# Zero products taken out of two attentions of a three-block network on one core

## The chip, the core and the metric

The kernel runs on one NeuronCore of one Trainium2 chip. Five engines matter: TensorE (PE) multiplies, VectorE (DVE) and ScalarE (ACT) work element by element, GpSimd (POOL) does a few additions and fills, and SyncE (SP) issues the loads. The metric is the device time of one execution in microseconds; the lower the better. The time of the kernel before is 1631.91 us, the median of three runs.

## What is computed

A sequence of 256 positions and 1024 channels passes a first block of two layers (an even mixer of convolutions, an odd mixer of a linear recurrence and a dilated attention, each followed by a gated feed-forward) and a second block of two layers (feed-forward, a mixer of pooling and a latent attention, feed-forward). All numbers are 32 bits wide. Cut to what the change touches:

```python
def dilated_attention(q, k, v, q_norm_g, k_norm_g):      # once, in the odd layer
    for g, (window, dilation) in enumerate(((128, 1), (512, 4), (2048, 16))):
        o, lse = dilated_group_attention(qn[:, :, g], kn[:, :, g], vr[:, :, g], window, dilation)
    ...
    out = jnp.einsum("gbsh,gbshd->bshd", softmax(lses), outs)

def mla_attention(...):                                   # twice, in each layer of the second block
    s = (einsum('bhqd,bhkd->bhqk', qn_b, kn) + einsum('bhqd,bkd->bhqk', qr_b, k_rope)) * SOFTMAX_SCALE
    s = jnp.where(qpos[:, None] >= kpos[None, :], s, -jnp.inf)
    p = jax.nn.softmax(s, axis=-1)
    return jnp.einsum('bhqk,bhkd->bhqd', p, vv)
```

## The kernel before

Activations stay in the core's memory; 343 MB of weights stream past them. Every unit of weights (mostly 128 x 2048 numbers) is loaded into `raw`, copied by ACT to a rounded high part `wh` and subtracted by DVE to a low part `wl`, and PE multiplies with both. Each engine has its own program, written out by hand; semaphores order them, and within an engine the work runs in the order in which it is written. Nothing is scheduled by a planner.

The dilated attention runs in three rounds: round 0 is the first 128 positions with four heads, rounds 1 and 2 are the second 128 positions with two heads each. Per round the stations are:

- `scores(r)` on PE, line 824: 6 products of 128 x 256 or 12 of 128 x 128;
- on DVE the mask (line 1705), the row maximum (line 1712) and its negative (line 1713);
- on ACT the exponentials (line 1191); on DVE the reciprocal (line 1723) and the scaling (line 1726), which give the probabilities;
- `turn(r)` on PE, line 835: 12 transposes; on ACT the copy of what they give (line 1201);
- `values(r)` on PE, line 846: 12 products of probabilities and values; on ACT the copy of the result (line 1348).

PE's program runs them as scores 0, half a unit of the output projection (line 738), scores 1, turn 0, scores 2, values 0, turn 1, values 1, turn 2, values 2, then the rest of the output projection (lines 738 and 646). DVE works through mask 1, probabilities 1, the low part of one weight unit (line 1490), mask 2, probabilities 2.

The latent attention has two rounds with the same stations (its mask is line 1708, its last copy line 1442). There half units of the output projection stand between the stations: scores 1, turn 0, half a unit, values 0, half a unit, turn 1, values 1, half a unit and the rest.

The function `spin(n, bk)` (line 671) multiplies a 128 x 128 tile of zeros `ZB` (16-bit numbers) with itself four times side by side, n times over, into a bank of the accumulator memory that is written afresh afterwards. Nothing reads what it writes. It is called in two places at the beginning (8 and 14 products), ahead of values 0, 1 and 2 of the dilated attention (3, 4 and 4 products) and ahead of values 1 of each latent attention (3 products), 39 in all. The spin calls in the attentions stand in front of the wait of `values` for ACT's copy (`_turned`).

Of the kernel before, what the change touches and what calls it, by code (L numbers as in the profile page):

```python
# [261 lines left out]
def build(nc, A, const, out):  # L262

    ctx = ExitStack()
    with ctx:
# [43 lines left out]
        def bank(i, a=0, n=512, rows=slice(0, P)):  # L309
            return PS[rows, i, a:a + n]  # L310
# [15 lines left out]
        def pairs(ap, w=S):  # L326
            return ap.rearrange("p (t s) -> p t s", s=w)

        def over(ap, n):

            return ap.unsqueeze(1).to_broadcast([ap.shape[0], n, ap.shape[1]])
# [38 lines left out]
        def ev(name):  # L370

            if name not in events:
                events[name] = sem("ev_" + name)
            return events[name]
# [229 lines left out]
        def _(pe):  # L604
# [66 lines left out]
            def spin(n, bk=5):  # L671

                for _ in range(n):
                    mm(pairs(bank(bk), P), lhsT=ZB[:], rhs=over(ZB[:], 4), start=True, stop=True)
# [279 lines left out]
            scores(1)  # L954
            turn(0)
            scores(2)
            spin(3, 7)
            values(0)
            turn(1)
            pe.wait_ge(ev("dil_taken"), 1)  # L960
            spin(4, 7)
            values(1)
            turn(2)
            pe.wait_ge(ev("dil_taken"), 2)
            spin(4, 7)
            values(2)
            half_unit(od, 6, "y_od", True, 6)
            for u in range(1, 4):
# [4 lines left out]
            for l in range(2):  # L973
# [65 lines left out]
                half_unit(n0 + 1, 5, fill, False)  # L1039
                turn(1)  # L1040
                pe.wait_ge(ev("y_pool"), 4 * l + 4)
                spin(3, 7)
                values(1)
                half_unit(n0 + 2, 6, fill, False)
                for u in range(3):
# [1117 lines left out]
```

## Time and profile before

| | |
|---|---|
| median of the runs | 1631.91 us (1629.73, 1631.91, 1632.4) |
| the profiled execution | 1632.11 us, of which its span is 1630.3 us |
| PE busy | 1595.9 us, 98% of the span |
| DVE busy | 1262.8 us, 77% |
| ACT busy | 854.8 us, 52% |
| mean granted clock of PE | 0.997 |
| zero products in the trace | 39, of them 22 at the beginning, 11 in the dilated attention (from 444.9 us), 3 in each latent attention |

The span is the time from the first to the last instruction; 1.81 us of the profiled execution lie around it. The granted clock is 1.00 at 2.4 GHz and 0.50 at 1.2 GHz. A busy PE in the profile has its matmuls overlapping: one of 12 that follow each other is shown with its whole latency, so the pace is read from where the next group starts. In the trace a product of two 32-bit tiles has two records, hence x24 for 12 products, while transposes have one each.

### The profile page before, as it was taken

To read this page: it belongs to the slowest core of one execution; us is meant where nothing else is said; L and a number is where in the kernel's file an instruction comes from. 1 tells how busy PE (TensorE), PEld (TensorE's weight loads), DVE (VectorE), ACT (ScalarE), POOL (GpSimd) and SP (SyncE) were. 2 spreads that over 40 slices of the span, in tenths; PEclk is the share of its full clock that TensorE was granted. 3 is DMA by queue.
4 is the path that set the end of the run, shared out by engine and by line. 5 is a ranking of instruction groups with operands and counts; after the bars stand their busy time and mean duration, and the time that the engine had idled before them with its cause. 6 is when DMAs were issued, how large, how long until landed. Compare 5 with 4: busy or idle time off the path is not lost.

```text
span 1630.3 us, 26968 instructions
## 1 busy us (share of the span) xinstructions
PE 1595.9 (98%) x11041; PEld 1453.5 (89%) x11041; DVE 1262.8 (77%) x1449; ACT 854.8 (52%) x1025; POOL 56.7 (3%) x76
## 2 busy tenths in 40 slices
PE   8999999999989999999999999999999999999998
PEld 7989999888789999899999799999899998899997
DVE  6977889886768898778888777885878888685555
ACT  5556645555356554654446565444644455564443
POOL 3001000000010000000000010000000000010000
PEclk9999999999999999999999999999999999999999
DMA  7514888744236886488974348876498854266562
GB/s 246 181 52 155 298 316 292 254 152 136 65 128 235 324 290 197 140 291 309 306 249 141 128 140 305 305 259 193 140 320 316 309 182 159 80 192 194 180 189 82
DMA packets 231438, 343.65 MB, mean 211 GB/s; under 512 B 7066, under 2 KB 194048, under 8 KB 231360
## 3 DMA queue, kind: packets, MB, share of 16 engines
q1 hardware_dynamic: 230304, 341.11, 62.0%
q0 software_dynamic: 752, 1.18, 0.2%
q8 instruction: 55, 0.90, 0.2%
q10 hardware_dynamic: 304, 0.27, 0.1%
q14 instruction: 23, 0.19, 0.0%
HBM read 341.48 MB, written 1.05 MB: 210 GB/s over the span
## 4 chain that ended last, share of the span: by engine, by line
PE 76%; DVE 11%; issue 5%; ACT 5%; SPq 1%; DMA 0%; DVEq 0%; ACTq 0%
PE PS L666 21%; PE PS L768 20%; PE PS L667 11%; PE PS L646 9%; PE PS L624 4%; DVE wl L1490 4%; PE PS L738 2%; ACT wh L1069 2%; PE PS L633 2%; PE PS L694 2%; PE PS L895 2%; DVE Z L1589 1%; DVE XL L1506 1%; PE PS L824 1%; SPq L521 1%
## 5 line engine op out<-in xcount | busy, mean ns | idle before, releaser
L1490 DVE TENSOR_TENSOR wl<-raw,wh 128x2048 fp32r<-128x2048 f32 (+2 forms) x256 | 570.4, 2231 | 153.5 <-ACT wh L1069 151.5
L666 PE MATMUL PS<-HP,wh 128*128 128x512 f32 x1728 | 607.8, 395 | 0.0
L1069 ACT ACTIVATE wh<-raw 128x2048 fp32r<-128x2048 f32 (+2 forms) x256 | 475.6, 1859 | 139.9 <-PE PS L768 117.0
L667 PE MATMUL PS<-HP,wl 128*128 128x256 f32 x1728 | 484.2, 280 | 0.0
L666 PEld LDWEIGHTS PS<-HP,wh 128*128 128x128 f32 x1728 | 324.1, 188 | 74.7 <-DVE wl L1490 0.3
L768 PE MATMUL PS<-FX,wh 128*128 128x256 f32 x1920 | 345.1, 281 | 1.8 <-DVE FX L1655 1.8
L667 PEld LDWEIGHTS PS<-HP,wl 128*128 128x128 f32 x1728 | 326.4, 189 | 0.0
L768 PEld LDWEIGHTS PS<-FX,wh 128*128 128x128 f32 x1920 | 294.7, 188 | 4.4 <-DVE wl L1490 2.0
L768 PE MATMUL PS<-FX,wl 128*128 128x256 f32 x960 | 269.9, 281 | 0.0
L768 PEld LDWEIGHTS PS<-FX,wl 128*128 128x128 f32 x960 | 180.7, 188 | 0.0
L1589 DVE SCALAR_TENSOR_TENSOR Z<-ada,CA,Z 128x1024 f32 x126 | 161.3, 1280 | 1.3
L646 PE MATMUL PS<-HP,wh 128*128 128x256 f32 x848 | 156.9, 287 | 3.0 <-issue 1.9
L624 PE MATMUL PS<-FX,wh 128*128 128x258 f32 (+2 forms) x576 | 142.2, 286 | 5.5 <-ACT FX L1081 3.6
L646 PEld LDWEIGHTS PS<-HP,wh 128*128 128x128 f32 x848 | 133.6, 194 | 9.4 <-issue 4.7
L624 PE MATMUL PS<-FX,wl 128*128 128x258 f32 (+2 forms) x576 | 140.0, 282 | 0.0
L1135 ACT ACTIVATE WK<-PS 128x512 f32<-128x512 f32 x54 | 32.3, 598 | 197.0 <-PE PS L667 197.0
L646 PE MATMUL PS<-HP,wl 128*128 128x256 f32 x424 | 119.3, 284 | 0.0
L624 PEld LDWEIGHTS PS<-FX,wh 128*128 128x128 f32 (+1 forms) x576 | 108.1, 188 | 10.5 <-ACT FX L1081 5.3
L624 PEld LDWEIGHTS PS<-FX,wl 128*128 128x128 f32 (+1 forms) x576 | 108.2, 188 | 0.0
L1160 ACT ACTIVATE WK<-PS 128x512 f32<-128x512 f32 x54 | 32.0, 593 | 97.0 <-PE PS L667 96.9
L646 PEld LDWEIGHTS PS<-HP,wl 128*128 128x128 f32 x424 | 81.7, 193 | 0.0
L633 PE MATMUL PS<-XL,wh 128*128 128x256 f32 (+1 forms) x576 | 75.5, 283 | 0.0
(281 smaller groups left out, 1724.5 us busy)
## 6 DMA issues: line engine op xcount, KB each, us to landing
ada<-ada_w SPq DMA_DIRECT2D x144, 512.0 KB, 6.2
raw<-ffn_w_gate SPq DMA_DIRECT2D x66, 1024.0 KB, 5.4
raw<-ffn_w_up SPq DMA_DIRECT2D x66, 1024.0 KB, 5.5
raw<-ffn_w_down SPq DMA_DIRECT2D x66, 1024.0 KB, 5.0
raw<-od_w_in SPq DMA_DIRECT2D x13, 1024.0 KB, 5.3
raw<-ev_w_in SPq DMA_DIRECT2D x10, 1024.0 KB, 7.2
raw<-w_in SPq DMA_DIRECT2D x8, 1024.0 KB, 5.4
raw<-w_out SPq DMA_DIRECT2D x8, 1024.0 KB, 6.1
```

Source lines behind the costliest of these rows:

```text
L624: mm(bank(dst + m, 0, width, slice(0, rows[m])), lhsT=w(a, k, m * P, rows[m]), rhs=XH[:, k, 0:width], start=k == 0 and a == 0, stop=False, ...
L633: last = mm(bank(dst + m, 0, S, slice(0, rows[m])), lhsT=w(0, k, m * P, rows[m]), rhs=XL[:, k, :], start=False, stop=k == KD - 1, skip_gro ...
L646: last = mm(dst, lhsT=lhs(a, k), rhs=rhs(b, k), start=first and i == 0, stop=first and i == len(order) - 1, skip_group_check=not first)
L666: mm(pairs(bank(bk)), lhsT=lhs(0, k), rhs=HP[:, k], start=k == 0, stop=False, skip_group_check=True)
L667: last = mm(bank(bk, 0, S), lhsT=lhs(1, k), rhs=HH[:, k, :], start=False, stop=k == k_tiles - 1, skip_group_check=True)
L694: last = mm(bank(bk + h, 0, 512, slice(0, 4)), lhsT=cn("pick")[:, 3 - v:7 - v], rhs=Z[:, at + v * D + 512 * h:at + v * D + 512 * h + 512], ...
L738: last = mm(bank(bk, m * S, S), lhsT=w(a, k, m * P, P), rhs=H[b][:, k, :], start=m == 0 and k == 0 and i == 0, stop=False, skip_group_chec ...
L768: last = mm(bank(m // 2, (m % 2) * S, S), lhsT=w(a, k, m * P, P), rhs=rhs(b, k), start=begins and i == 0 and m % 2 == 0, stop=False, skip_ ...
L895: mm(bank(4 + t // 2, (t % 2) * S, S), lhsT=DG[:, i % DIAGS, :], rhs=cols(Z, EV["U"], 4, 30 + S)[:, t, k:k + S], start=k == DVE_TAPS, stop ...
L1069: last = A_(dst(wh), src, ACT.Copy)
L1490: last = tt(dst(wl), src, dst(wh).bitcast(F32), ALU.subtract)
L1589: ins = stt(total, w, CA[:, k:k + 1], total, ALU.mult, ALU.add)
```

## The change

Five calls of `spin` go: those before values 0, 1 and 2 of the dilated attention and the one in the loop over the two latent attentions. The 22 zero products at the beginning stay. Waits, orders and all other instructions stay as they are.

```diff
@@ dilated attention, PE
             scores(1)
             turn(0)
             scores(2)
-            spin(3, 7)
             values(0)
             turn(1)
             pe.wait_ge(ev("dil_taken"), 1)
-            spin(4, 7)
             values(1)
             turn(2)
             pe.wait_ge(ev("dil_taken"), 2)
-            spin(4, 7)
             values(2)
             half_unit(od, 6, "y_od", True, 6)
@@ latent attention, PE, in the loop over two layers
                 half_unit(n0 + 1, 5, fill, False)
                 turn(1)
                 pe.wait_ge(ev("y_pool"), 4 * l + 4)
-                spin(3, 7)
                 values(1)
                 half_unit(n0 + 2, 6, fill, False)
```

On PE in the dilated attention the row of instructions changes as follows (`PS` is the accumulator memory, `CN` holds the identity for transposes, `WK` the probabilities, `Z` queries, keys and values, `ZB` the zeros):

```order
 L835 MATMUL PS<-CN,WK 128x128 x12
 L824 MATMUL PS<-Z 128x256 x6
-L674 MATMUL PS<-ZB 128x512 x3
 L846 MATMUL PS<-WK,Z 64x128 x12
 L835 MATMUL PS<-CN,WK 128x128 x12
-L674 MATMUL PS<-ZB 128x512 x4
 L846 MATMUL PS<-WK,Z 64x128 x12
 L835 MATMUL PS<-CN,WK 128x128 x12
-L674 MATMUL PS<-ZB 128x512 x4
 L846 MATMUL PS<-WK,Z 64x128 x12
```

Three groups of zero products are gone, one in front of each `values`; nothing else has moved. On PE in each latent attention one group is gone between turn 1 and values 1 (`HP` holds the activations of the output projection):

```order
 L738 MATMUL PS<-HP,wl 128x256
 L835 MATMUL PS<-CN,WK 128x128 x8
-L674 MATMUL PS<-ZB 128x512 x3
 L846 MATMUL PS<-WK,Z 128x128 x8
 L738 MATMUL PS<-HP,wh 128x256 x2
```

The transposes are now followed directly by the products of the values, which wait for ACT's copy of the transposes.

## Rows read from the trace of the kernel before

**Rows 1.** The page: the span, and the shares of the chain that ended last.
```profile
span 1630.3 us, 26968 instructions
...
PE 76%; DVE 11%; issue 5%; ACT 5%; SPq 1%; DMA 0%; DVEq 0%; ACTq 0%
```

**Rows 2.** Zero products after 100 us: ns min/median/max, first and last start.
```profile
L674 PE MATMUL PS<-ZB x17: 379/379/379, 445.1 to 1412.0; 128*128 128x512 bf16 x17
```

**Rows 3.** Timeline, PE, dilated attention: start us, length us, what, [idle before <- releaser].
```profile
434.01 2.75 PE L824 MATMUL PS<-Z 128*128 128x256 f32 x12
439.41 1.97 PE L835 MATMUL PS<-CN,WK 128*128 128x128 f32 x12 [2.65 <-DVE WK L1726]
441.18 4.06 PE L824 MATMUL PS<-Z 128*128 128x256 f32 x12
445.08 0.81 PE L674 MATMUL PS<-ZB 128*128 128x512 bf16 x3
445.82 1.80 PE L846 MATMUL PS<-WK,Z 128*64 128x128 f32 x24
447.55 1.53 PE L835 MATMUL PS<-CN,WK 128*128 128x128 f32 x12
448.92 1.03 PE L674 MATMUL PS<-ZB 128*128 128x512 bf16 x4
450.62 2.46 PE L846 MATMUL PS<-WK,Z 128*64 128x128 f32 x24 [0.68 <-ACT WK L1201]
455.12 1.53 PE L835 MATMUL PS<-CN,WK 128*128 128x128 f32 x12 [2.04 <-DVE WK L1726]
456.49 1.03 PE L674 MATMUL PS<-ZB 128*128 128x512 bf16 x4
458.19 2.46 PE L846 MATMUL PS<-WK,Z 128*64 128x128 f32 x24 [0.68 <-ACT WK L1201]
462.56 0.47 PE L738 MATMUL PS<-HP,wh 128*128 128x256 f32 x2 [1.92 <-DVE HP L1556]
```

**Rows 4.** Timeline, ACT, dilated attention: the three copies of the transposes.
```profile
441.42 1.45 ACT L1201 ACTIVATE WK<-PS 128x1536 f32<-128x1536 f32 x1 [3.72 <-PE PS L835]
...
449.12 1.45 ACT L1201 ACTIVATE WK<-PS 128x1536 f32<-128x1536 f32 x1 [1.08 <-PE PS L835]
...
456.69 1.45 ACT L1201 ACTIVATE WK<-PS 128x1536 f32<-128x1536 f32 x1 [2.85 <-PE PS L835]
```

**Rows 5.** Timeline, DVE, dilated attention: between probabilities 1 and probabilities 2.
```profile
446.29 1.75 DVE L1490 TENSOR_TENSOR wl<-raw,wh 128x1536 fp32r<-128x1536 f32 x1
447.96 1.75 DVE L1705 TENSOR_TENSOR WK<-PS,CN 128x1536 f32<-128x1536 f32 x1
...
453.91 1.15 DVE L1726 TENSOR_SCALAR WK<-WK,SM 128x768 f32<-128x768 f32 x2
```

**Rows 6.** Windows of PE: stretch, length, busy (instructions), granted clock, DMA share, GB/s.
```profile
440.00:444.00 4.00, 4.00 (x16) 0.57 0.00 0
...
452.00:456.00 4.00, 1.96 (x20) 1.00 0.17 56
456.00:460.00 4.00, 3.32 (x30) 1.00 0.00 0
```

**Rows 7.** Timeline, latent attentions: round 1 of the first, then of the second.
```profile
933.85 0.81 PE L674 MATMUL PS<-ZB 128*128 128x512 bf16 x3
...
935.13 2.05 PE L846 MATMUL PS<-WK,Z 128*128 128x128 f32 x16 [0.47 <-ACT WK L1201]
...
1411.52 0.81 PE L674 MATMUL PS<-ZB 128*128 128x512 bf16 x3
1411.72 1.02 ACT L1201 ACTIVATE WK<-PS 128x1024 f32<-128x1024 f32 x1 [2.67 <-PE PS L835]
...
1412.80 2.05 PE L846 MATMUL PS<-WK,Z 128*128 128x128 f32 x16 [0.47 <-ACT WK L1201]
```

**Rows 8.** Windows behind the dilated attention: busy of PE, PEld, DVE, ACT, POOL; granted clock.
```profile
463.00:473.00 10.00, 10.00 (x86) 10.00 (x85) 6.31 (x7) 6.07 (x9) 2.02 (x2) 1.00 0.34 107
```

## The prediction

> **What bounds the kernel now.** I read the page first: the span is 1630.3 us, and the chain that ended last lies on PE for 76% of it [rows 1]. So PE's work counts where PE waits for nobody, and the question for each of the 17 zero products taken out [rows 2] is whether the engine had something else to do at that moment. The timeline of PE through the dilated attention tells that [rows 3]: behind the second and third group of zero products PE still sits idle for 0.68 us until ACT has copied the transposes, and in the latent attentions it sits idle for 0.47 us behind its group [rows 7]. Then I read the timelines of ACT and DVE beside it [rows 4, 5], which say what ends each wait, and last the granted clock in the windows [rows 6], since PE's clock is what such products can influence without anybody reading them. Behind the attention PE runs without a gap (10.00 of 10.00 us busy [rows 8]), so whatever delays the start of the output projection at 462.56 us is passed on whole.
>
> **The price of one zero product.** Three in a row take 0.81 us and each has 0.379 us of latency [rows 2, 3], so the pace is (0.81 - 0.379) / 2 = 0.216 us. Four in a row give (1.03 - 0.379) / 3 = 0.217 us. Seventeen are 17 x 0.216 = 3.7 us of PE; that they were all on the path would be the most the removal could give.
>
> **Group 1, ahead of values 0 (3 products).** ACT's copy for values 0 ended at 441.42 + 1.45 = 442.87 us [rows 4], long before values 0 started at 445.82 us. So this group really holds PE up: without it values 0 starts where the zeros started, at 445.08 us, 0.74 us earlier, and turn 1 at 446.81 instead of 447.55 us. Its probabilities are ready for that, because DVE goes on to its next work at 446.29 us, at the end of them [rows 5]. ACT's copy, which started at 449.12 us, then starts about 1.6 us (449.12 - 447.55) behind turn 1, at 448.38, and ends at 449.83 us; values 1 can start at 449.88 instead of 450.62 us. What is late next? Turn 2 waits for probabilities 2, and these come from a chain on DVE and ACT that starts with the mask at 447.96 us, directly behind the low part of a weight unit that starts at 446.29 us [rows 5]. The mask needs scores 2, which ended before 445.3 us (441.18 + 4.06) [rows 3], and nothing in it waits for values 0, turn 1 or values 1. So turn 2 stays at 455.12 us, and the 0.74 us end as idle time of PE. The term is 0.
>
> **Groups 2 and 3, ahead of values 1 and 2 (4 products each).** Values 2 starts at 458.19 us, directly behind ACT's copy (456.69 + 1.45 = 458.14 us [rows 3, 4]). The zeros ended at 457.52 us, beside that copy. Removing them changes nothing on the path: turn 2 (455.12), copy (456.69), values 2 (458.19), the last copies, projection (462.56) keep their times. The same for group 2, with 450.57 us as the end of the copy. The term is 0 for both; the cover is ACT's copy of 1.45 us against 0.87 us of zeros.
>
> **Latent attentions (3 products each).** The copy ends at 1411.72 + 1.02 = 1412.74 us and values 1 starts at 1412.80 us, while the zeros were over at 1412.33 us [rows 7]. The first layer has the same rows around 934 us, with the same 0.47 us of idle time. The term is 0 for both, and PE is idle there from the start of the copy to values 1 instead, 1412.80 - 1411.72 = 1.1 us, between projections on either side.
>
> **The clock.** Taken so far the sum is 0, and what remains is what the zeros do to the clock. In this trace it fell to 0.57 in the window 440 to 444 us, that is to the 1.2 GHz level for most of it [rows 6], right behind an idle time of 2.65 us in front of turn 0 [rows 3]. It did not fall in the windows of 452 to 460 us [rows 6], where the idle times are 0.68, 2.04, 0.68 and 1.92 us [rows 3]. The change opens just these: values 1 moves forward by 0.74 us while turn 2 stays, so the idle time before turn 2 becomes 2.04 + 0.74 = 2.78 us, longer than the 2.65 us that stood before the fall; the waits for ACT's copy become 458.19 - (455.12 + 1.53) = 1.54 us instead of 0.68. From the end of turn 1 to the projection PE then works for 2.46 + 1.53 + 2.46 = 6.45 us of about 14.2. One more fall here is therefore possible in many executions, and this trace can't say in which.
>
> Its price: at half the clock scores 2 took 4.06 us where the same products at 434.01 us took 2.75, so 1.31 us; turn 0 took 1.97 us where turn 1 and turn 2 took 1.53, so 0.44 us; together 1.75 us [rows 3]. There it cost nothing, since DVE's mask came at 447.96 us only, 2.7 us behind scores 2. In round 2 the work between waits is on the path. The ends are 0 (no further fall, or one that falls into idle time) and 1.75 us for each one, at most two of them between 452 and 470 us, 3.5 us. I take 0.44 us, the excess of turn 0, because the work that stands right behind the lengthened idle time is a turn of the same form, and because a good part of a slow stretch lies in waits. Below nothing there is no clock term: the one fall of before is off the path.
>
> The Trainium skill speaks against the change (TensorE: Matmul & The Clock Gate, section "HAM oscillation — how this bites in real kernels"): bursts of matmuls with waits between them lose the full clock again and again, and the extra time is the throttled time multiplied by (1 - 1.2/2.4). The rows agree on the size: 4.06 + 1.97 us of slowed work cost 1.75 us, of which not all ran slow. By that rule every thinned attention would pay; this is the second rival below.
>
> **The sum.** 1632.11 us of the profiled execution, plus 0 for the five groups, plus 0.44 us for the clock, is 1632.5 us. The profiled execution stands 0.2 us above the median of 1631.91 us, so no correction is worth making.
>
> **Rivals.** (1) The zeros were holding nothing, and the clock falls no more often than before. For it: the clock stayed at 1.00 over 2.04 and 1.92 us of idle time; against it: 2.78 us is beyond the 2.65 us behind which it fell in this attention. The time is 1632.1 us. (2) Slower: the clock falls twice or more on the path. The place is round 2 of the dilated attention and the start of the projection, with idle times of 2.78, 1.54 and 1.92 us close to each other, and perhaps the latent attentions too. Two falls give 1632.1 + 3.5 = 1635.6 us, three 1637.4 us. It decides from the second full fall on. Against it: in the latent attentions only 1.1 us of idle time opens between dense work, and any slow stretch after 462.56 us is met by the dense work of the projection, and dense work is what lifted the clock again here after the fall at 440 us: it was at 1.00 by 452 us [rows 6]. (3) Faster: the zeros did stand in the way, because the next real product isn't free to start while they drain, or because executions differ in when ACT's copy ends. All 17 on the path give 0.74 + 2 x 0.87 + 2 x 0.65 = 3.8 us and 1628.3 us. Against it speak four idle times behind the zeros, 0.68 and 0.47 us, in front of the very products that would be freed [rows 3, 7].
>
> **How the numbers follow.** The forecast, hidden zeros and at most one fall on the path, has 0.66, rival 1 has 0.18, rival 2 has 0.11, rival 3 has 0.05. A measurement of this kernel can tell about 0.2% from no change, that is 3.3 us; forecast and rival 1 lie within it. Of rival 2 I count 0.10 as slower by more than that, of rival 3 0.04 as faster, and 0.86 remain. The range goes down to the lowest run of before, 1629.7 us, since nothing but rival 3 is below it, and up to two falls, 1635.6 us.
>
> **What the profile after would show.** Values 0 follows scores 2 directly. The idle time before turn 2 longer, near 2.8 us, and turn 2 still released by DVE line 1726. Values 2 and both late `values` of the latent attentions released by ACT line 1201, with idle times near 1.5 and 1.1 us. The stretch from probabilities 1 to the start of the output projection (446.3 to 462.56 us, 16.3 us) unchanged where the clock stays at 1.00, longer by up to 1.75 us where it shows 0.50. The forecast is wrong if the projection starts earlier relative to probabilities 1, or if the clock is low in two or more places where it was full before.

## The result

The changed kernel takes 1635.86 us, the median of 12 executions (1632.15 to 1639.27), beside 1632.34 us for the kernel before in the same series (12 executions, 1629.73 to 1636.66). The ratio is 1.0019 with a 95% interval of 1.0010 to 1.0028: slower by about 0.2%. Two more series of the same kernel gave 1.0001 (0.9991 to 1.0011) and 1.0000 (0.9987 to 1.0012). Taken together the mean of 35 executions of the changed kernel is 1634.7 us and that of 98 of the kernel before is 1633.6 us, so the removal costs 1.1 us, with a 95% interval of 0.2 to 2.0 us. This leans on the first series: one by one the means differ by 3.5, 0.4 and 0.3 us, and the last two alone don't tell the removal from nothing. In the first series the kernel before also had only one of 12 executions above 1634.5 us, against 33 of 86 in the others. Four executions of over 1700 us (one of the changed kernel, three of the kernel before) are left out of all means here.

The profiled execution of the changed kernel took 1633.50 us, with this span on the page, to be held against [rows 1]:

```profile
span 1631.7 us, 26936 instructions
```

The timeline of PE through the dilated attention (start us, length us, what, [idle before <- releaser]) answers to [rows 3]. The line numbers of ACT and DVE are lower by four than before, as the calls are gone.

```profile
433.55 2.75 PE L824 MATMUL PS<-Z 128*128 128x256 f32 x12
438.96 2.47 PE L835 MATMUL PS<-CN,WK 128*128 128x128 f32 x12 [2.66 <-DVE WK L1722]
441.22 3.54 PE L824 MATMUL PS<-Z 128*128 128x256 f32 x12
444.69 1.80 PE L846 MATMUL PS<-WK,Z 128*64 128x128 f32 x24
446.42 1.53 PE L835 MATMUL PS<-CN,WK 128*128 128x128 f32 x12
449.54 2.43 PE L846 MATMUL PS<-WK,Z 128*64 128x128 f32 x24 [1.58 <-issue]
454.88 1.53 PE L835 MATMUL PS<-CN,WK 128*128 128x128 f32 x12 [2.91 <-DVE WK L1722]
457.99 2.43 PE L846 MATMUL PS<-WK,Z 128*64 128x128 f32 x24 [1.59 <-issue]
462.33 0.48 PE L738 MATMUL PS<-HP,wh 128*128 128x256 f32 x2 [1.92 <-DVE HP L1552]
```

Values 0 follows scores 2 directly, the three zero groups have become idle time, and turn 2 still waits for DVE. The idle times of 1.58 and 1.59 us are put down to `issue` and not to ACT, but ACT's copy ends right before each: the last one starts at 456.44 us and takes 1.45, which is 457.89 us, 0.10 us before values 2. From scores 1 to the output projection it is 462.33 - 433.55 = 28.78 us, where it was 462.56 - 434.01 = 28.55 us before [rows 3]. Up to there the removal of 11 products has changed 0.23 us, and to the worse. The stretch that the prediction named, from the end of probabilities 1 to the projection, starts with this line of DVE:

```profile
446.05 1.75 DVE L1486 TENSOR_TENSOR wl<-raw,wh 128x1536 fp32r<-128x1536 f32 x1
```

It is 462.33 - 446.05 = 16.28 us, before it was 462.56 - 446.29 = 16.27 us [rows 3, 5]: unchanged. What follows is new. The windows of PE (stretch, length, busy and records, granted clock, DMA share, GB/s) right behind the start of the projection, which [rows 8] shows at 1.00 throughout:

```profile
462.00:464.00 2.00, 1.67 (x11) 0.82 0.03 8
464.00:466.00 2.00, 2.00 (x12) 0.50 0.00 0
466.00:468.00 2.00, 2.00 (x16) 0.83 0.00 0
468.00:470.00 2.00, 2.00 (x19) 1.00 0.33 68
```

PE starts 12 matmuls in 2 us at the lower clock against 19 at the full one. What that costs is seen at the first product behind the output projection, before and then after:

```profile
477.03 0.28 PE L624 MATMUL PS<-FX,wh 128*128 128x256 f32 x1
```
```profile
478.30 0.28 PE L624 MATMUL PS<-FX,wh 128*128 128x256 f32 x1
```

From the start of the projection it took 477.03 - 462.56 = 14.47 us, now it takes 478.30 - 462.33 = 15.97 us: the fall of the clock cost 1.50 us. The values 1 of the latent attentions come here:

```profile
936.50 2.02 PE L846 MATMUL PS<-WK,Z 128*128 128x128 f32 x16 [1.21 <-ACT WK L1197]
...
1414.19 2.02 PE L846 MATMUL PS<-WK,Z 128*128 128x128 f32 x16 [1.21 <-ACT WK L1197]
```

Against [rows 7] they are late by 936.50 - 935.13 = 1.37 and 1414.19 - 1412.80 = 1.39 us. Between the two nothing more was lost. Of the 1.37 us, 1.27 were there at 478.30 us already, and the other 0.1 us is new in the latent attention: values 1 starts 0.15 us behind the end of ACT's copy, where it was 0.06 us. The spans differ by 1.4 us. In this pair of executions the changed kernel reached scores 1 0.46 us earlier, lost 0.23 us in the attention, 1.50 us to the fall in the projection, and 0.1 us in the latent attention.

### The profile page after: what moved, and what is told of

Its sections match the earlier page's. It is cut to its first block, busy times and chain, and to the rows that moved or that the text cites. A ratio compares the mean times of both kernels' runs of the same rounds, so it can differ in the third digit from the quotient of the medians.

```text
span 1631.7 us, 26936 instructions
## 1 busy us (share of the span) xinstructions
PE 1592.5 (98%) x11024; PEld 1453.7 (89%) x11024; DVE 1263.1 (77%) x1449; ACT 854.7 (52%) x1025; POOL 56.6 (3%) x76
## 3 DMA queue, kind: packets, MB, share of 16 engines
HBM read 341.48 MB, written 1.05 MB: 210 GB/s over the span
## 4 chain that ended last, share of the span: by engine, by line
PE 76%; DVE 11%; issue 5%; ACT 5%; SPq 1%; DMA 0%; DVEq 0%; ACTq 0%
PE PS L666 21%; PE PS L768 20%; PE PS L667 11%; PE PS L646 9%; PE PS L624 4%; DVE wl L1486 4%; PE PS L738 2%; ACT wh L1065 2%; PE PS L633 2%; PE PS L694 2%; PE PS L895 2%; DVE Z L1585 1%; DVE XL L1502 1%; SPq L521 1%; PE PS L824 1%
```

## The experiments

Theory: the removed products were hidden behind waits and cost nothing, and what they did was to keep PE's clock full; without them it falls more often at places of the path. Rivals: the latent attentions pay as well; the difference has nothing to do with the clock; the zeros hold nothing. Besides the medians, each execution's mean clock is used.

**One part alone.** The label dil_only leaves the 11 products of the dilated attention out:

```diff
-            spin(3, 7)
             values(0)
...
-            spin(4, 7)
             values(1)
...
-            spin(4, 7)
             values(2)
```

> Only the 11 zero products of the dilated attention are taken out, the 6 of the latent attentions stay. Theory (clock falls in the dilated attention and at the start of its output projection): the whole slowing of the change is here, 2.5 to 4 us above the kernel before, and the runs have a lower mean clock, 0.991 to 0.996. Rival (the latent attentions pay too): 1 to 2 us, about half. Rival (something else than the clock, such as the placement of the code): a difference of time without one of the clock.

Measured: 1633.86 us, ratio 1.0002 (0.9992 to 1.0013), mean 1634.3 against 1633.6 us. The size was missed. The clock went from 0.991 to 0.997, but its mean, 0.9946 against 0.9954, is hardly lower; one of 12 executions (1639.39 us, 0.991) has a lower clock and a longer time than any of the kernel before. The label lat_only leaves out the other 6:

```diff
                 pe.wait_ge(ev("y_pool"), 4 * l + 4)
-                spin(3, 7)
                 values(1)
```

> Only the 6 zero products of the latent attentions are taken out, the 11 of the dilated attention stay. Theory: no difference from the kernel before, within 1 us, since only 1.1 us of idle time opens there between dense stretches. Rival (the latent attentions pay too): 1 to 2 us slower, with falls of the clock near 935 or 1413 us in some executions.

Measured: 1633.04 us, ratio 0.9994 (0.9985 to 1.0004). The means differ by 0.1 us with an uncertainty of 1.1 us, no execution stands out, and in the profile the clock is 1.00 around both latent attentions. So they pay nothing that can be measured here.

**The changed kernel again.**

> The changed kernel once more, for a second profile and for each run's mean clock beside its time. Theory: 2.5 to 4 us above the kernel before, and run by run the time rises by about 1.6 us for each 0.001 that the mean clock is lower (0.001 of 1632 us), since every slowed product is on the path. Rival (the extra time has nothing to do with the clock): no such relation.

Measured: 1633.24 us, ratio 1.0001; the size was missed again. The relation held in kind: over the 12 executions the time rises by 1.05 us for each 0.001 of mean clock, in the first series by 1.26 us, and by 1.26 and 1.20 us over 35 and 31 executions of the kernel before. The executions of the changed kernel of 1638.67 us and above all have a clock of 0.991. The code is the same in each of these, so its placement doesn't make their difference.

> The changed kernel a third time, for a tighter comparison. So far its medians stood 3.5 and 0.05 us above the kernel before in two series. Theory (the removal costs nothing where the clock is full, and lets it fall once more on the path in a part of the executions): a mean 0.5 to 2 us above the kernel before, the fastest execution no faster or slower than that of before by over 0.5 us, and now and then an execution with a mean clock of 0.991, which the kernel before doesn't show. Rival (no effect at all, the first series was chance): equal means within 0.5 us and equal clocks.

Measured: 1634.21 us, ratio 1.0000, mean 1634.3 against 1634.0 us, which is below the expected rise and doesn't exclude the rival by itself. One execution had a clock of 0.991 (1638.98 us). Its profiled execution gives the clearest view of the cost, because the clock fell at nearly the same moments as in that of lat_only, which has the zeros of the dilated attention. PE's timeline of the changed kernel in this execution:

```profile
436.35 2.75 PE L824 MATMUL PS<-Z 128*128 128x256 f32 x12
...
457.84 1.69 PE L835 MATMUL PS<-CN,WK 128*128 128x128 f32 x12 [3.08 <-DVE WK L1722]
461.12 4.56 PE L846 MATMUL PS<-WK,Z 128*64 128x128 f32 x24 [1.59 <-issue]
467.60 0.47 PE L738 MATMUL PS<-HP,wh 128*128 128x256 f32 x2 [1.92 <-DVE HP L1552]
```

and of lat_only:

```profile
436.49 2.75 PE L824 MATMUL PS<-Z 128*128 128x256 f32 x12
...
457.88 1.53 PE L835 MATMUL PS<-CN,WK 128*128 128x128 f32 x12 [2.36 <-DVE WK L1725]
459.25 1.85 PE L674 MATMUL PS<-ZB 128*128 128x512 bf16 x4
461.03 3.26 PE L846 MATMUL PS<-WK,Z 128*64 128x128 f32 x24
...
466.21 0.48 PE L738 MATMUL PS<-HP,wh 128*128 128x256 f32 x2 [1.92 <-DVE HP L1555]
```

The windows of the same two kernels, first without and then with zeros:

```profile
460.00:464.00 4.00, 2.88 (x18) 0.50 0.00 0
464.00:468.00 4.00, 2.08 (x11) 0.76 0.00 0
```
```profile
460.00:464.00 4.00, 4.00 (x26) 0.66 0.00 0
464.00:468.00 4.00, 2.08 (x18) 1.00 0.01 4
```

In both the clock fell near 459 us. (It had fallen near 442 us in both as well, and turn 2 starts 0.3 to 0.4 us later behind scores 1 than before in either.) With the zeros it was back before values 2 was through (3.26 us); without them it stayed low and values 2 took 4.56 us. From scores 1 to the projection it is 31.25 us without and 29.72 us with zeros, 1.5 us on the path, where an undisturbed passage takes 28.55 us. In this one pair, then, the zeros didn't prevent the fall, and the lower clock lasted longer without them.

**Which group.** The label g23_only leaves out only the two groups of four:

```diff
             pe.wait_ge(ev("dil_taken"), 1)
-            spin(4, 7)
             values(1)
...
             pe.wait_ge(ev("dil_taken"), 2)
-            spin(4, 7)
             values(2)
```

> Only groups 2 and 3 of the dilated attention (4 and 4 zero products, behind ACT's copies) are taken out; group 1 ahead of values 0 and the 6 of the latent attentions stay. Theory (groups 2 and 3 matter, since they halve the waits around turn 2): the idle time before turn 2 is near 2.0 to 2.4 us, and executions with a clock of 0.991 and over 1637.5 us appear as with the changed kernel, in 1 of 8 or so. Rival (it is group 1, which lengthened the idle time before turn 2 to 2.9 us): none of these, and a mean equal to the kernel before within 0.5 us.

Measured: 1637.16 us, ratio 1.0012 (0.9999 to 1.0025), mean 1636.0 against 1634.0 us, with an uncertainty of 1.8 us for the difference; 6 of 12 executions above 1637 us. The idle time before turn 2 in its profile:

```profile
457.82 1.53 PE L835 MATMUL PS<-CN,WK 128*128 128x128 f32 x12 [2.26 <-DVE WK L1724]
```

So the loss needs no lengthened idle time there. Its windows show where the loss sits, in the projection again:

```profile
464.00:466.00 2.00, 0.72 (x6) 1.00 0.00 0
466.00:468.00 2.00, 2.00 (x12) 0.56 0.05 8
468.00:470.00 2.00, 2.00 (x13) 0.59 0.00 0
470.00:472.00 2.00, 2.00 (x20) 1.00 0.06 8
```

From the projection's start to the first product behind it (465.28 to 481.24 us) it is 15.96 us, 1.5 us more than before, as in the changed kernel. Over the executions the sharpest count is this: of 59 executions without groups 2 and 3 (the three series of the changed kernel, dil_only, this one) 14 took more than 1637 us, of 109 with them (the kernel before and lat_only) none, and the highest was 1636.91 us. The line of 1637 us was drawn after the times were known, but the count doesn't hang on one series: it is 4 of 12 against 0 of 12, 2 of 24 against 0 of 46, 2 of 11 against 0 of 31, and 6 of 12 against 0 of 20. Group 1 alone wasn't tried; that it matters not at all is not shown.

**More zeros in the same places.** The label quad17 multiplies each group by four, leaving nothing out (the comments are added here):

```diff
-            spin(3, 7)        # ahead of values 0
+            spin(12, 7)
-            spin(4, 7)        # ahead of values 1 and values 2
+            spin(16, 7)
-                spin(3, 7)    # in each latent attention
+                spin(12, 7)
```

> Each group of the removed zeros four times as long instead: 12, 16 and 16 in the dilated attention, 12 in each latent attention. Nothing is left out. This measures the cover from the other side. By the cover read in the trace (1.5 us ahead of values 2, 1.1 us ahead of the late values of each latent attention): values 2 comes 16 x 0.216 - 1.54 = 1.9 us later, with what group 1 and 2 push into turn 2 about 3.4 us; each latent attention 12 x 0.216 - 1.1 = 1.5 us; 5 to 7 us together. Rival (zeros are on the path from the first on): 51 x 0.216 = 8.4 us for the 39 added and 17 old ones beyond the changed kernel. Rival (they never are): 0.

Measured: 1639.26 us, 4.95 us above the median before (ratio 1.0033, 1.0021 to 1.0046); the means differ by 5.7 us, where 5 to 7 were expected. PE's timeline in its profile:

```profile
436.18 2.75 PE L824 MATMUL PS<-Z 128*128 128x256 f32 x12
...
460.31 3.62 PE L674 MATMUL PS<-ZB 128*128 128x512 bf16 x16
...
468.22 0.48 PE L738 MATMUL PS<-HP,wh 128*128 128x256 f32 x2 [1.91 <-DVE HP L1556]
```

The stretch from scores 1 to the projection is 468.22 - 436.18 = 32.04 us, 3.49 us more than 28.55; 3.4 were expected. (From scores 2 to values 2 PE waits for nothing here, so the slow scores 2 of a fall near 442 us, 3.48 us long, counts in the stretch; the rows from which the forecast was made had such a fall too.) In each latent attention values 1 comes 3.46 us behind turn 1 instead of 2.15, so 1.3 us later, where 1.5 were expected. The rival by which every zero costs falls (its 8.4 us is a slip: the 51 added products at 0.216 us are 11.0 us), and so does that by which none ever does. The cover read from the trace has about its size.

This profile also shows what the zeros don't do. The clock fell in the projection here too, with four times the zeros in front of it:

```profile
468.00:470.00 2.00, 1.78 (x12) 0.81 0.00 0
470.00:472.00 2.00, 2.00 (x11) 0.50 0.00 0
```

The projection again took 1.5 us longer, and over the eight executions the clock was 0.994 to 0.997, no better than that of the kernel before. Why it fell here is not shown.

**Zeros in other places.** The label fill keeps all and adds 25:

```diff
             scores(1)
+            spin(10, 7)
             turn(0)
...
             values(1)
+            spin(8, 4)
             turn(2)
...
             values(2)
+            spin(7, 4)
             half_unit(od, 6, "y_od", True, 6)
```

> All zero products stay, and 25 more fill the three longest idle times of the dilated attention: 10 ahead of turn 0, 8 ahead of turn 2, 7 ahead of the output projection (2.2, 1.7 and 1.5 us into 2.65, 2.04 and 1.92 us). Theory: no fall between 436 and 480 us, scores 2 takes 2.75 us instead of 4.06, and the median is 1 to 2 us below the kernel before, because its executions with a fall on the path are gone. Rival (zero products hold nothing): falls as before and the same median. Rival (they delay real work): slower by up to 1 us.

Measured: 1632.71 us, ratio 0.9995 (0.9987 to 1.0004), the mean clock 0.9974 against 0.9954. In its profile scores 2 took 2.86 us, at the full clock, and there is no fall from 436 to 480 us. The gain of 1 to 2 us was missed: the mean fell by 0.3 us only, with an uncertainty of 1.0 us. A likely reason, not tested alone, is that the fall that is gone is mostly the one near 440 us, and that one lay beside DVE's work. The label moved has the same 25 and none of the 17:

> The 17 removed zero products stay out, but 25 stand in the longest idle times of the dilated attention instead: 10 ahead of turn 0, 8 ahead of turn 2, 7 ahead of the output projection. Theory (it is the idle time before the clock looks that counts, not the 17 places): no fall between 436 and 480 us in the profile, the same mean as with the label fill, 1633.3 us, within 0.5 us. Rival (the old places are needed as well): falls in the waits for ACT's copies and a mean like that of the changed kernel.

Measured: 1632.82 us, ratio 0.9996 (0.9986 to 1.0006), mean 1633.2 us, as with fill (1633.3). Windows of PE in its profile:

```profile
440.00:444.00 4.00, 3.37 (x21) 1.00 0.00 0
444.00:448.00 4.00, 3.98 (x31) 1.00 0.00 0
448.00:452.00 4.00, 2.13 (x21) 1.00 0.00 0
...
456.00:460.00 4.00, 2.28 (x16) 1.00 0.00 0
```

There is no fall from 436 to 480 us, although the waits for ACT's copies stand empty as in the changed kernel, and no execution was above 1635.42 us. The 17 places are not the only ones that will do.

**A version that beats both.** The label all_fill adds, to fill, 22 zeros in the first mixer:

```diff
             first_units(U0["ev_in"], "mix0")
+            pe.wait_ge(z_out, 1)
+            spin(5, 0)
...
+                        if fill == "mix0" and k == 4 and b == 0:
+                            spin(3, 1)
                         pe.wait_ge((hh_ready, h_ready)[b], FILL[fill] + k // 2 + 1)
...
+            spin(5, 7)
             pe.wait_ge(ev("cf_conv"), 2)
...
             last.then_inc(ev("ln_sum"), 1)
+            spin(9, 4)
             pe.wait_ge(ev("ln_sq"), 1)
```

> The zeros of the label fill, and 22 more ahead of waits in the first mixer: 5 and 3 around the fourth unit of its input projection (near 33 and 36 us), 5 ahead of the sum and 9 ahead of the squared sum of its layer norm (near 104 and 107 us). Theory (every fall in these waits costs up to 1.7 us where dense work follows, and zeros hold the clock): clock 0.997 to 0.999, no execution above 1634 us, a mean 1 to 2 us below the kernel before. Rival (the zeros cost on the path as much as they save): a mean within 0.5 us.

Measured: 1632.92 us (1631.21 to 1634.06), ratio 0.9993 (0.9983 to 1.0002), mean 1.3 us lower, clock 0.997 to 1.000.

> The kernel of the label all_fill once more, since its interval (0.9983 to 1.0002) didn't settle a gain of about 1.3 us in the mean. Theory (zeros in the waits keep the clock full and the spread of executions small): again no execution above 1634.5 us, and a mean 1 to 2 us below the kernel before. Rival (chance of one series): a mean within 0.5 us of the kernel before.

Measured: 1631.56 us (1630.36 to 1634.34), ratio 0.9987 (0.9978 to 0.9996), mean 1631.7 against 1634.0 us, 2.3 us lower, a little more than was forecast. PE's windows in the kernel before and then in this one:

```profile
34.00:38.00 4.00, 2.21 (x13) 0.95 0.77 246
38.00:42.00 4.00, 4.00 (x24) 0.63 0.30 104
```
```profile
34.00:38.00 4.00, 3.91 (x26) 1.00 0.65 203
38.00:42.00 4.00, 4.00 (x33) 1.00 0.39 132
```

At 38 to 42 us PE is busy in both, with 24 matmuls in one and 33 in the other: that is what a fall in front of dense work takes. But this pair doesn't show that the zeros there prevented it. In the profiles of dil_only and after_again, which have no zeros at that place, these windows stand at 1.00 too, and as in this one the clock had fallen at 12 to 20 us instead. What the zeros did is seen over the executions: in the 23 of both series none has a clock below 0.997 or a time above 1634.34 us, and in neither profile does the clock fall near 110 us or near 440 us, as it does in most of the others. Which of the added groups brought the gain is open.

## Why the prediction was right, and where it was not

**The price of a zero product and its cover: right.** The idle times behind the removal are 2.91, 1.58 and 1.59 us in the dilated attention and 1.21 us in the latent ones, where 2.78, 1.54, 1.54 and 1.1 us were forecast. None of the 17 was on the path: the stretch to the projection didn't get shorter, the one from probabilities 1 kept its 16.3 us, and quad17 measured the cover by overrunning it. Rival 3 (faster) falls with this.

**The latent attentions at nothing: right**, by lat_only and by the equal lateness of 1.37 and 1.39 us at both, but for 0.1 us by which values 1 now follows the copy later.

**The clock: right in kind, the term mis-sized.** I took 0.44 us, the excess of one turn, because I set the likely fall in front of turn 2 and took a good part of it as hidden. Measured over 35 and 98 executions the term is 1.1 us (0.2 to 2.0), and it isn't one small cost in every execution but a full one in some. In the profile after, the fall stood in the output projection, where all of it is on the path, and cost 1.50 us, near the upper price of 1.75 us; g23_only and quad17 show the same 1.5 us; the pair of after_third and lat_only gives 1.5 us for a longer low clock. The first series stood 3.5 us above the kernel before, its median 0.26 us beyond the upper end of the range, and by it alone rival 2 (1635.6 us) would have been the better forecast; that the other two series came out near 0.44 us is luck as much as insight. The upper end of the range was two falls, and the spread of the executions was not in it: those of the changed kernel alone go from 1631.56 to 1639.27 us, by where the clock happens to fall.

**"Below nothing there is no clock term", since the fall near 440 us was off the path: nearly right.** Where that fall catches turn 0 whole, it isn't free. Turn 0 took 2.47 us in the profile after instead of 1.97, so ACT's copy, at 441.47 us, started 0.51 us later behind scores 1 than before, and the exponentials of round 1 right behind it 0.23 us later.

**The idle time before turn 2 as the point of decision: wrong.** I argued with 2.78 us against 2.65. g23_only lost most with 2.26 us there, and lat_only fell near 459 us behind 2.36 us, with the zeros in place. A single idle time compared with another said nothing here. That it is the filling of the waits from turn 1 to the projection as a whole fits g23_only, fill and moved, but quad17's profile speaks against a simple rule of this kind.

**The two remaining rivals.** That the zeros held nothing had 0.18; 14 of 59 against 0 of 109 speak against it, though the medians of the second and third series don't. That two falls or more decide towards slower had 0.11; single executions do that (1638 to 1639 us, clock 0.991), and the first series as a whole, but not the mean over all three. The prediction's own sign of being wrong, a low clock in two or more places where it was full before, didn't come in the profile after: there is one such place.

The Trainium skill (TensorE: Matmul & The Clock Gate, section "HAM oscillation — how this bites in real kernels") puts the extra time at the throttled time multiplied by (1 - 1.2/2.4); worked out from it as an estimate, 0.001 of mean clock over 1632 us is 1.63 us. In the series of the changed kernel and of the kernel before the time rose by 1.05 to 1.26 us for it, about two thirds to three quarters, as part of a low stretch can lie in waits. The clock is on record to 0.001 only, and one small series (moved, 12 executions) gives 1.9 us, so this is rough. In these series the rule's price is too high for a kernel whose PE waits.

## What to carry to other kernels

An instruction whose result nobody reads and that runs inside a wait has next to no price, and its effect must be looked for in the clock: first ask what its engine does in the whole stretch of waits around it, and then which work stands behind, since a fall in dense work was paid in full here (1.5 us) and one beside another engine's chain hardly at all (0 to 0.4 us). Filling the long waits of the attention and of the first mixer together was worth 0.1% here; filling those of the attention alone was worth nothing that could be measured. Where executions of one kernel differ by several microseconds by the place of a fall, three of them decide nothing about a change of one; count the extreme ones as well as the median.

## What was unexpected about the hardware

The falls come at other moments in every execution of the same code: near 37, 110, 440 and 459 to 466 us in some profiles, near 14 us in others, near 322 us in one, and the same kernel before gave 1629.73 and 1636.91 us. Much of this spread has nothing to do with the change: the profiled execution of moved took 1635.42 us without a fall from 436 to 480 us, but with a clock of 0.60 and 0.54 at 36 to 44 us and 0.58 at 112 to 116 us. At the lower clock the zero products take part in the slowness themselves (four of them 1.85 us in lat_only instead of 1.03 us), still hidden by the copy but for less than 0.1 us. And zeros as operands are enough to keep the clock up: with 47 more of them than before, in waits all over the first mixer and the attention, its mean stood at 0.997 to 1.000 over the whole execution, against 0.993 to 0.997.
